# Two reordered queues in the mixers of a hybrid diffusion step

## The reference, cut to what matters

```
h = rms_norm(x) * (1 + scale) + shift
proj = h @ w_in                       # latents of q and kv, rotary key, lru_x, lru_gate, merge gates
q = rms_norm(q_lat) @ w_q_up;  ckv = rms_norm(kv_lat);  kv = ckv @ w_kv_up
xc = centred_conv(lru_x)
for each of two directions:           # 8 chunks of 128 channels
    r, i = sigmoid(block_diag(xc)), sigmoid(block_diag(xc))
    log_a = -8 * softplus(-lambda) * r
    u = sqrt(-expm1(2 * log_a)) * i * xc
    h_t = exp(log_a) * h_(t-1) + u_t  # a scan over the tokens
y = (gates1 * mla + gates2 * ((hf + hb) * gelu(lru_gate)) @ w_o_lru) @ w_out
```

## Time and profile before

| what | value |
|---|---|
| median of 3 runs | 1281.16 us (1281.06 to 1282.22) |
| the profiled execution, its own time | 1280.97 us |
| its span, first to last instruction | 1278.9 us |
| mean granted clock of TensorE | 0.997 |
| PE busy | 1242.3 us (97%) |
| DVE busy | 836.5 us (65%) |
| ACT busy | 658.0 us (51%) |
| DMA | 156 GB/s mean |

### The profile page before, as it was taken

The page is one execution under the profiler, slowest core; times in us unless marked ns, Lnnn a source line. Parts: engine busy times, 40 slices in busy tenths (PEclk is TensorE's granted clock), DMA queues, the critical chain, the costliest instruction groups (busy, mean ns, idle before and its releaser), DMA issues.

```text
span 1278.9 us, 19550 instructions
## 1 busy us (share of the span) xinstructions
PE 1242.3 (97%) x7457; PEld 1145.8 (90%) x7457; DVE 836.5 (65%) x1382; ACT 658.0 (51%) x1161; POOL 18.4 (1%) x41
## 2 busy tenths in 40 slices
PE   6999999999999999999999999999999999999998
PEld 4899999978879999998879998998798899999886
DVE  2697684764868877749768795756566884343423
ACT  5479873754454333342255989557445533333322
POOL 0000000200000000000000000011000000000000
PEclk9999999999999999999999999999999999999999
DMA  9645555333346766548824334263325464444451
GB/s 335 211 135 160 184 163 196 106 116 115 113 134 213 230 208 220 166 135 274 271 63 139 103 108 116 84 232 115 100 76 164 154 201 129 132 132 132 157 165 49
DMA packets 132128, 199.34 MB, mean 156 GB/s; under 512 B 10330, under 2 KB 70980, under 8 KB 132036
## 3 DMA queue, kind: packets, MB, share of 16 engines
q1 hardware_dynamic: 132036, 198.11, 48.7%
HBM read 196.16 MB, written 1.92 MB: 155 GB/s over the span
## 4 chain that ended last, share of the span: by engine, by line
PE 78%; DVE 10%; ACT 7%; issue 2%; DMA 1%; SPq 1%; DVEq 0%; ACTq 0%
PE bank L718 16%; PE bank L725 16%; PE bank L726 16%; PE bank L837 6%; PE bank L838 6%; PE bank L839 6%; DVE weight_low L1651 3%; ACT weight_high L1269 2%; ACT sq L1277 1%; PE bank L1137 1%; DVE lru_h L1939 1%; PE bank L1161 1%; DVE lru_tau L1943 1%; PE bank L755 1%; DVE lru_i L1935 1%
## 5 line engine op out<-in xcount | busy, mean ns | idle before, releaser
L725 PE MATMUL bank<-act_low,weight_high 128*128 128x384 f32 x1440 | 487.7, 339 | 3.6 <-DVE weight_low L1651 3.6
L726 PE MATMUL bank<-act_high,weight_low 128*128 128x384 f32 x1440 | 482.6, 335 | 0.0
L1651 DVE TENSOR_TENSOR weight_low<-raw,weight_high 128x1024 fp32r<-128x1024 f32 (+5 forms) x282 | 319.8, 1152 | 168.8 <-ACT weight_high L1269 168.4
L1269 ACT ACTIVATE weight_high<-raw 128x1024 fp32r<-128x1024 f32 (+5 forms) x282 | 273.0, 995 | 224.7 <-DMA raw<-in_w_ffn_out 62.5
L718 PE MATMUL bank<-act_high,weight_high 128*128 128x384 f32 x1440 | 315.1, 339 | 4.4 <-ACT sq L1360 2.7
L725 PEld LDWEIGHTS bank<-act_low,weight_high 128*128 128x128 f32 x1440 | 271.3, 188 | 10.9 <-DVE weight_low L1651 5.8
L726 PEld LDWEIGHTS bank<-act_high,weight_low 128*128 128x128 f32 x1440 | 271.3, 188 | 0.0
L718 PEld LDWEIGHTS bank<-act_high,weight_high 128*128 128x128 f32 x1440 | 253.6, 188 | 12.0 <-issue 4.7
L837 PE MATMUL bank<-weight_high,hid_high 128*128 128x512 f32 x264 | 103.2, 391 | 0.0
L839 PE MATMUL bank<-weight_high,hid_low 128*128 128x512 f32 x264 | 102.8, 389 | 0.0
L838 PE MATMUL bank<-weight_low,hid_high 128*128 128x512 f32 x264 | 102.8, 389 | 0.0
(11 more groups left out here) (262 smaller groups left out, 1473.3 us busy)
## 6 DMA issues: line engine op xcount, KB each, us to landing
raw<-in_w_ffn_in SPq DMA_DIRECT2D x176, 256.0 KB, 3.9
mod_weight<-in_w_mod SPq DMA_DIRECT2D x80, 512.0 KB, 4.8
raw<-in_w_in SPq DMA_DIRECT2D x72, 512.0 KB, 4.0
raw<-in_w_ffn_out SPq DMA_DIRECT2D x44, 512.0 KB, 4.5
first_mod<-in_w_mod SPq DMA_DIRECT2D x4, 2048.0 KB, 14.2
raw<-in_w_o_lru SPq DMA_DIRECT2D x16, 512.0 KB, 3.7
raw<-in_w_out SPq DMA_DIRECT2D x16, 512.0 KB, 3.7
raw<-in_w_o_mla SPq DMA_DIRECT2D x8, 512.0 KB, 5.0
```

Source lines behind the costliest of these rows:

```text
L725: nc.tensor.matmul(o, view[0][:, kk, cols], low[:, k, :], start=False, stop=False)
L726: ins = nc.tensor.matmul(o, view[1][:, kk, cols], high[:, k, :], start=False, stop=k == total - 1)
L1269: nc.scalar.activation(high, w, ACT.Copy).then_inc(*AC.step())
L1651: nc.vector.tensor_tensor(low, w, high.bitcast(F), ALU.subtract).then_inc(*VE.step())
```

## The change

Nothing is computed differently; instructions of ACT and of DVE trade places.

On ACT, in the first half's coefficients, the high part of gg1's first load moves ahead of step 7, and the four gate-input copies move from behind the loop to step 8, ahead of the last root. In the second half's coefficients the high parts of m2a3 and of m2b0 to m2b3 are made after steps 0, 1, 3, 4 and 6, where they were made after 1, 3, 5, 7 and 9; the inverse roots move from behind step 5 to step 2, ahead of the root of that step.

On DVE, the low part of gg1's first load moves ahead of `squared_roots(3)`; `xc_low(6)` and the low parts up to gates1's second load come right after `scans(3)`, ahead of `gated(4)`, and the latent sums move behind the low part of gg1's last load. The low part of m2a3 moves ahead of `squared_roots(4)`, that of m2b0 ahead of `squared_roots(5)`, that of m2b1 ahead of `scans(4)`, that of m2b2 behind `squared_roots(6)`, and that of m2b3 ahead of `squared_roots(7)` and of the normalised latents.

```diff
+                        if b == 1 and e == 2:
+                            ac.wait_ge(*at(PE, "latent_norms"))
+                            inverse_root("q", bank("st_qkv", 0), QL, sq[0])
+                            inverse_root("kv", bank("st_qkv", 1), KVL, sq[1])
+                        if b == 0 and e == 8:
+                            gate_inputs_out()
                         if e >= 2 and e % 2 == 0:
...
-                        if b == 1 and e == 5:
-                            ac.wait_ge(*at(PE, "latent_norms"))
-                            inverse_root("q", bank("st_qkv", 0), QL, sq[0])
-                            inverse_root("kv", bank("st_qkv", 1), KVL, sq[1])
...
+                def gate_inputs_out():
+
+                    for c in range(4):
+                        ac.wait_ge(*at(PE, "gg0", c))
+                        nc.scalar.activation(ybuf[:, c, :], bank("gg0", c)[:, 0:T], ACT.Copy).then_inc(*AC.step("gate_input", c))
...
-                lru_coefficients(0, {1: ("gg0", 1), 3: ("gg0", 2), 5: ("gg0", 3), 7: ("gates1", 0)})
-                for c in range(4):
-                    ac.wait_ge(*at(PE, "gg0", c))
-                    nc.scalar.activation(ybuf[:, c, :], bank("gg0", c)[:, 0:T], ACT.Copy).then_inc(*AC.step("gate_input", c))
+                lru_coefficients(0, {1: ("gg0", 1), 3: ("gg0", 2), 5: ("gg0", 3), 6: ("gg1", 0), 7: ("gates1", 0)})
...
-                lru_coefficients(1, {1: ("m2a", 3), 3: ("m2b", 0), 5: ("m2b", 1), 7: ("m2b", 2), 9: ("m2b", 3)})
+                lru_coefficients(1, {0: ("m2a", 3), 1: ("m2b", 0), 3: ("m2b", 1), 4: ("m2b", 2), 6: ("m2b", 3)})
...
                 scans(1, 1)
+                lows("gg1", 0)
                 squared_roots(3)
                 lows("gates1", 0)
                 scans(2, 2)
                 lows("gg1", 1)
                 scans(3, 3)
+                xc_low(6)
+                lows("gates1", 1)
+                gated(4)
+                gated(5)
+                xc_low(7)
+                gated(6)
+                lows("gg1", 3)
 
                 ve.wait_ge(*at(AC, "sqq", QC + KC - 1))
...
-                gated(4)
-                xc_low(6)
-                lows("gates1", 1)
-                gated(5)
-                xc_low(7)
-                gated(6)
-                lows("gg1", 3)
                 gated(7)
                 lows("m2a", 2)
                 mod_partial(7)
+                lows("m2a", 3)
                 squared_roots(4)
-                lows("m2a", 3)
+                lows("m2b", 0)
                 squared_roots(5)
                 mod_result(6)
+                lows("m2b", 1)
                 scans(4, 0)
-                lows("m2b", 0)
                 squared_roots(6)
-                lows("m2b", 1)
+                lows("m2b", 2)
                 scans(5, 1)
+                lows("m2b", 3)
                 squared_roots(7)
-                lows("m2b", 2)
...
                 scans(6, 2)
-                lows("m2b", 3)
                 mod_partial(8)
                 lows("m1a", 0)
                 scans(7, 3)
```

## The result

Over 20 runs of each, the changed kernel took 1284.05 us and the kernel before 1281.33 us (medians); the ratio is 1.0018, with a 95% interval from 1.0010 to 1.0025. One of the 20 runs took 2473.66 us; the ratio leaves it out, the median does not (1283.85 us without it). The profiled execution took 1284.66 us, its span is 1282.9 us, and the mean granted clock 0.994.

What follows compares the result with a forecast made beforehand. PE, 97% busy, was taken as bound, with a second bound from the end of `scans(7)` to m1a1. Losses of 3.15 us (first layer) and 0.14 (second) gave +3.3 us, forecast 1284.5 us, range 1281.9 to 1286.4.

Steps and rivals of the forecast that it cites:

- PE's waits in the mixers vanish: Both mixers: PE's waits for low parts and inverse roots go, 2.6 and 5.65 us, together 8.3 us.
- ACT's entry into the second half's coefficients: ACT starts these coefficients earlier by the PE waits removed: 0.96 us in the first layer, 2.2 us in the second.
- The latent sums fill the idle time: On DVE, the moved latent sums fall where it idled 1.52 us for ACT's sigmoids and cost nothing.
- Second layer: ACT spends its 2.2 us on the inverse roots; `scans(7)` ends 0.13 us later, net +0.14 us.
- First layer: ACT waits for m2b0's load and DVE's run ends later; PE loses 0.65 + W, 3.15 us.
- W: ACT's wait for m2b0's raw load in the first layer's second-half coefficients: 1.3 to 3.5 us, taken as 2.5.
- the two rows that I had: Earlier profile rows: the third queued load lands 6.6 or 8.8 us after the first issue.
- the slack of 0.35 us at m1a1: First layer, before the change: m1a1's low part ends at 194.31 and PE takes it up at 194.66.
- a wait at the second load of m1a: Sign: new PE waits of 2 us and more at the first two loads of m1a in both layers.
- A load in time: First layer: m2b0's load delays ACT by at most 0.6 us; +0.8 to +1.4 us, 1282.3; chance 0.12.
- PE keeps its gain: DVE's run starts earlier, at `a(5,1)` on ACT, so `scans(7)` ends sooner; 1272.9 us for all 8.3; chance 0.08.
- TensorE's clock: The clock falls in PE's wait at m1a, some 1.6 us of matmuls a fall; 1286 to 1287 us; chance 0.13.

Runs made afterwards that it cites:

- the load ahead: Changed kernel with m2b0's load put ahead of the two modulation blocks in SP's queue: 1281.92 us, ratio 1.0005 to the kernel before.
- second half alone: Changed kernel with the edits before the second half's coefficients put back, those from there on kept: 1287.59 us, ratio 1.0041 to the kernel before.
- roots at step 3: Changed kernel with the inverse roots behind the high part of step 3 instead of in step 2: 1283.12 us, ratio 1.0027 to the kernel before.
- roots at step 5: Changed kernel with the inverse roots behind step 5, as before the change: 1283.52 us, ratio 1.0016 to the kernel before.
- m1a ahead: Changed kernel with the high and low parts of m1a1 and m1a2 made ahead of scans(7): 1281.38 us, ratio 0.9999 to the kernel before.
- the first half alone: Changed kernel with only the edits up to the second half's coefficients kept, the rest put back: 1277.87 us, ratio 0.9979 to the kernel before.
- the fastest version: Changed kernel with m2b0's load and m1a1/m1a2 parts ahead, inverse roots behind step 3, m2b2's high part behind step 5: 1273.61 us, ratio 0.9946.
- all three remedies: Changed kernel with m2b0's load ahead of modulation blocks, m1a1/m1a2 parts ahead of scans(7), inverse roots behind step 3: 1275.73 us, ratio 0.9967.
- the kernel before with m1a ahead: Kernel before, with only the high and low parts of m1a1 and m1a2 made ahead of scans(7): 1280.4 us, ratio 1.0001.

## Why the prediction was right

In what follows times of the changed kernel are set against those of the kernel before by taking off the 0.32 us (first layer) or 2.19 us (second) by which PE was already late where the mixer starts.

**PE's waits in the mixers vanish and PE comes to m1a 5.6 us sooner in the second layer.** Shown: 3.43 + 2.19 = 5.62 us.

**ACT's entry into the second half's coefficients.** Forecast 155.50 and 780.85. Measured 155.89 - 0.32 = 155.57 and 783.14 - 2.19 = 780.95. (The terms written out for the first layer add up to 0.94 us, not 0.96; it changes nothing.) The latent sums fill the idle time of the earlier trace rows: `gated(4)` starts at 143.54, without a pause in front of it, where it was 144.55 behind 1.52 us of idle time.

**Second layer.** ACT's timeline, against the earlier trace rows: its instructions follow each other in the order that was summed, and the last line is the end of pair `a(5,1)`:

```profile
783.14 0.62 ACT L1445 ACTIVATE t<-lru_r,lam 128x384 f32<-128x384 f32 x1
...
788.10 0.56 ACT L1360 ACTIVATE sq<-bank,epsc 128x384 f32<-128x384 f32 x1
...
790.15 0.92 ACT L1458 ACTIVATE lru_tau<-lru_tau,epsc 128x768 f32<-128x768 f32 x1
...
792.36 0.60 ACT L1446 ACTIVATE lru_r<-lru_r,lam 128x384 f32<-128x384 f32 x1
```

It ends 9.82 us after the start (9.83 forecast). DVE's run starts at 793.95 - 2.19 = 791.76 (791.68) and ends at 816.27 (816.24). Net +0.16 (+0.14).

**First layer.** W was 2.14 us, in its range of 1.3 to 3.5 and below the 2.5 chosen: the third of three queued loads landed 7.9 us after the first issue, between the two rows that I had. With it the run should end at 191.7 + 2.14 = 193.84; it ended at 194.25 - 0.32 = 193.93. The term mis-sized the other way is the slack of 0.35 us at m1a1. I let PE use it all up. After, the low part ended at 197.84 and PE took it up at 198.06, so 0.22 us were left over. That is not a cost of handing over. Where PE did wait for this low part it started 0.05 us after its end: 820.82 + 1.23 = 822.05 and 822.10 in the second layer, and likewise in the first layer of the run with the load ahead. Here PE was late by itself, through the low clock from 188 us on: that cost up to 0.17 us. 0.65 + 2.14 = 2.79 forecast with the measured W, 3.08 measured; the error in the slack (0.2) and the end of the run (0.1) made up for most of the error in W (0.36). The net of 3.08 against 3.15 is closer than its parts.

One sign that was forecast did not show in the first layer: a wait at the second load of m1a. PE's wait at the first load is 3.4 us; the one at m1a1 (about 1.6 forecast) was filled by slow products. Only the second layer has both.

W itself is not a fixed price. Five profiles have this order of loads. ACT waited 2.14 us (the whole change), 2.21 (second half alone), 2.69 (roots at step 3), 2.10 (roots at step 5) and 0.43 (m1a ahead), and took the block up 6.6 to 8.0 us after the first of the three issues. The value of one profile is partly chance.

The Trainium skill (DMA: Bandwidth & Descriptors, Anatomy of one DMA) would have given 5.6 us from first issue to last landing, as an estimate from its fixed cost and rate; this trace measured 7.9 us. The Trainium skill fits these numbers, in the same section, to transfers issued from GpSimd, and these were issued by SP. In none of the five profiles did it come down to 5.6 us.

**The sum.** By position in the traces +3.24 us (3.3 forecast). By the runs +2.3 us, interval 1.3 to 3.2. The chance of 0.63 on slower by more than 0.2% went to an outcome that is slower, by 0.18%. The two can differ by a microsecond because the position is that of one execution: W varies from one to the next, and so do the falls of the clock, below. Which of them it was is not shown.

**The rivals.** A load in time: not in this profile (W 2.14), but in one of the five (0.43), so some executions of the changed kernel may well be of that kind. PE keeps its gain: no; but the run of the first half alone, and the last one, show that it was near. If the second half's edits had left `scans(7)` alone, 1.8 us by position and 2.7 by the runs were there to be kept. TensorE's clock: it fell in m1a's wait in the first layer, as feared, and stayed low for 6.8 us, twice as long as in its other falls here. All engines from 188.40 and from 823.30 us, where the changed kernel has its other new fall; PEclk stands third from last:

```profile
188.40:195.20 6.80, 5.83 (x19) 5.86 (x20) 5.74 (x15) 0.92 (x3) 0.00 (x0) 0.52 0.27 77
823.30:826.80 3.50, 3.50 (x14) 3.50 (x13) 2.85 (x5) 2.78 (x3) 0.00 (x0) 0.56 0.46 143
```

Both are at the lower level, 1.2 GHz. The first stretch began in the wait of 3.4 us, 2.0 us after PE's last product, and cost PE at most 0.2 us, since PE would have waited in it for m1a1; the second cost 1.55 us, about the 1.6 told. By the Trainium skill (TensorE: Matmul & The Clock Gate, Why this matters for your kernels) idle gaps bring such falls; this trace agrees for the first stretch, inside 3.4 us of idle time. A wait of 2.4 us in the kernel before, in the earlier trace rows, brought none.

## What to carry to other kernels

A wait of the busiest engine is worth its time only if nothing else ends at the same moment further on. Look for the next engine that runs without a pause, follow its last output to where the busy engine takes it up, and read the slack there (0.3 us here, against 8.3 us of waits) before pricing the edit. When work moves ahead in one engine's order, ask of each moved piece whether its input is there (m2b0 stood behind two other transfers) and which output behind it is now later. And where a price hangs on when a transfer lands, one profile is one draw: the same wait measured 0.4 to 2.7 us here.

## What the runs showed that I had not expected

The time of one kernel follows the mean granted clock of the run closely. The kernel before, of 61 runs those at a clock with five or more:

| mean clock | runs | mean time |
|---|---|---|
| 0.998 | 16 | 1279.42 us |
| 0.997 | 14 | 1281.38 us |
| 0.995 | 19 | 1282.08 us |
| 0.994 | 5 | 1283.24 us |

About 0.9 us for each 0.001 of clock. From 0.994 to 0.998 that is 3.8 us, more than the whole effect studied. (0.001 of 1280 us would be 1.3 us, so part of the lost clock is not paid for.) Different orders have different mean clocks: 0.9965 for the kernel before and 0.9963 for the fastest version; 0.9944 for the change, 0.9943 with m1a ahead and with the second half alone and 0.9927 with the roots at step 5. The last four all have a PE wait of 2.2 us or more at m1a or m2b in both mixers, and the fastest version none above 1.0 there. The others lie between: 0.9948 with the roots at step 3 (waits of 2.8 and 2.4 us), 0.9949 with the load ahead (1.4 and 2.2), 0.9955 with the first half alone (1.4 and 2.4), 0.9958 with all three remedies (0.2 and 1.4, five runs) and 0.9962 for the kernel before with m1a ahead (1.1 and 2.4). This is why two versions with spans 4.6 and 7.6 us shorter than the change were only 0.3 and 2.4 us better by the ratios: a span is one execution, and these two were profiled at clocks of 0.995 and 0.998, above their own average. What a single run or profile says of an edit of a few microseconds here has to be read with its clock beside it. The eleven profiles also tell where the clock falls. They have 22 mixers. In 14 of them PE waits once for 2.2 us or more, and in 10 of these the clock falls in that wait or at most 2.1 us behind it; in the 8 mixers with shorter waits (1.4 us at most) it never falls. That the waits cause the falls is likely from both, but no run changed a wait alone; it is argued, not shown. It also stays open why the change at an equal clock is only some 0.6 to 2.1 us above the kernel before (lines fitted through the runs of each meet the mean clocks of 0.9944 and 1 at 1283.4 and 1280.0 us, against 1282.8 and 1277.9), and not 3.2: a fall that lies in a wait costs next to nothing (0.2 us at m1a above), and the change has more of both, which would fit.
